# Summing the conv norm's four feature tiles and four squares on VectorE before TensorE sums over partitions

## The chip, the cores and the metric

The kernel runs on one core of a Trainium2 chip. The metric is the device time of one launch in microseconds. Engines: TensorE (PE; its weight loads are PEld), VectorE (DVE), ScalarE (ACT), GpSimd (POOL) and SyncE (SP, whose queue issues the weight transfers). Names after "L" are line numbers of the kernel before.

## The reference

The program computes a first block, then a second block of two layers over 528 positions (16 meta tokens and 512 tokens) of 2048 features. Of each layer of the second block only this matters here:

```
c = c_val * jax.nn.sigmoid(c_glu)
c = _causal_depthwise_conv_2(c, conv_dw_w, conv_dw_b)
c = jax.nn.silu(_layer_norm(c, conv_ln_g, conv_ln_b))
c = c @ conv_pw_w + conv_pw_b
y_conv = c * jax.nn.silu(c_gate)
...
mixed = jnp.concatenate([y_conv, y_attn, y_lru], axis=-1) @ w_out
return _layer_norm(DEEPNORM_ALPHA * h + mixed, ln_post_g, ln_post_b)
```

`_layer_norm` over the 512 conv features takes a mean and then a variance of the centred values. Both are sums over features.

## The kernel before

Activations are held feature-major: a tile is 128 features on the partitions by 528 positions along the free axis, so the 512 conv features are four tiles, y2[:, Y_CONV + d] with d from 0 to 3. A sum over features is a sum over partitions and over four tiles. TensorE does it: `sum_features` (L740) multiplies each tile by a matrix of ones, in two halves of 264 positions, and adds the four tiles up in PSUM. These are plain fp32 matmuls. The large products run as three reduced-precision ones (high times high, low times high, high times low; L513 to L515).

The large products go by "units". A unit is 256 columns of a weight matrix by all positions. It has two passes (m = 0, 1) of four pieces (j = 0 to 3), and a piece in a layer is 24 matmuls of 264 positions. Its weights come by DMA to w_raw, ScalarE makes w_high of them (`high`, L979) and VectorE w_low (`low`, L1471). A piece of the next unit's w_high can be made only when the same piece of this unit's second pass is done (piece_used). Everything is ordered by hand: each engine has its own list, and semaphores join them. Extra work of TensorE is put between pieces by a hook that is called after each piece (n = 0 to 7 in a unit).

The order around the change, in each of the two layers:

- TensorE does unit C (O_CG, the last unit of the loop over groups). After its piece 6 comes the mean (`c_mean`), then piece 7. Then unit C + 1, with the variance (`c_var`) after its piece 0. Then the conv branch's pointwise product PW (L940 to L944), which waits until the normed conv tiles are ready (c_ready) and until all PSUM banks are free (evac), and then six units and a tail of the output product.
- VectorE ends the recurrence of the last group (L1992 to L2003), then `lows(C + 1, range(3))`, then subtracts the mean from the four tiles (L2012), `low(C + 1, 3)`, the reciprocal (L2015), the scaling (L2018) and c_low (L2021).
- ScalarE copies out unit C (L990), makes three pieces of w_high, squares the four centred tiles (L1393), makes the fourth piece, takes the root of the variance (L1397), then silu and c_high for four tiles (L1400, L1402), copies out unit C + 1's first pass (L990), then four times `high(C + 2, j)`, with three pieces of x_high (L1106) between, and then copies out unit C + 1's second pass. That last copy is the evac that PW waits for.

Of the kernel before, what the change touches and what calls it, by code (L numbers as in the profile page):

```python
# [22 lines left out]
ALU = mybir.AluOpType  # L23
# [24 lines left out]
CT = CW // P  # L48
TAPS = 31
HD = 64  # L50
NKV = 4
# [22 lines left out]
O_K, O_V, O_K2, O_GRP, O_CG, O_PW, O_OUT = 0, 1, 2, 3, 19, 21, 22  # L74
# [6 lines left out]
Y_ATT, Y_LRU, Y_CONV = 0, 8, 12  # L81
# [25 lines left out]
def program(nc, a, out):  # L107
# [14 lines left out]
    with ExitStack() as ctx:  # L122
# [92 lines left out]
        y2 = r2.take("y_layer", [P, KT, L])  # L215
# [48 lines left out]
        dif = rn.take("norm_difference", [P, L])  # L264
        dsq = rn.take("norm_square", [P, L])
# [3 lines left out]
        csq = nc.alloc_sbuf_tensor_at("c_square", [P, CT, L], F32, offset=big + 3 * CT * L * 4)  # L269
# [4 lines left out]
        def sem(name):  # L274
            return ctx.enter_context(nc.semaphore(name))
# [47 lines left out]
        c_taken, rw_in, r_conved, r_mm, r_act, r_act2, r_w, r_sqrt, lru_done, pads_ok = (  # L323
            sem("c_taken"), sem("rw_in"), sem("r_conved"), sem("r_mm"), sem("r_act"), sem("r_act2"), sem("r_w"), sem("r_sqrt"),
            sem("lru_done"), sem("pads_ok"))
        zeros_ok = sem("zeros_ok")
        c_gated, c_part, att_sum = sem("c_gated"), sem("c_part"), sem("att_sum")
        lam_exp, sp_ok = sem("lam_exp"), sem("sp_ok")
        cn_mean, cn_c, cn_sq, cn_mm, cn_rt, cn_t, cn_hi, c_ready = (
            sem("cn_mean"), sem("cn_c"), sem("cn_sq"), sem("cn_mm"), sem("cn_rt"), sem("cn_t"),  # L330
            sem("cn_hi"), sem("c_ready"))
# [177 lines left out]
        def _(pe):  # L509
# [29 lines left out]
            def unit(U, fill, wide=False, after=(None, None), mid=(None, None), hook=None, tok=slice(0, S)):  # L539

                for m in range(2):
                    begin(U, m)
                    for j in range(4):
                        arrive(U, m, j, fill)
                        for kt in range(4):
                            k = 4 * j + kt
                            if wide:
                                for q in range(2):  # L550
                                    last = three(ps[:, 2 * m + q, 0:LH], k, None, slice(q * LH, (q + 1) * LH), m, j, kt, k == 0, k == KT - 1)
                            else:
                                last = three(ps[:, m, :], k, None, tok, m, j, kt, k == 0, k == KT - 1)
                        end_piece(U, m, j, last)
                        if j == 1 and mid[m]:
                            mid[m]()
                        if hook:
                            hook(4 * m + j)
                    if after[m]:
                        after[m]()  # L560
# [24 lines left out]
            for d in range(KT):  # L585
                if d >= 4:
                    pe.wait_ge(tr_raw_free, d - 3)
                for i in range(ST):
                    last = pe.transpose(ps[:, 4 + d % 4, i * P:(i + 1) * P], xn[:, i, d * P:(d + 1) * P], ident[:])
# [5 lines left out]
            for d in range(KT):  # L595
# [4 lines left out]
                for i in range(ST):  # L600
                    last = pe.transpose(ps[:, 4 + d % 4, i * P:(i + 1) * P], xs[:, i, d * P:(d + 1) * P], ident[:])
# [5 lines left out]
            for h in range(H):  # L607
                last = pe.transpose(ps[:, 4 + h // 4, h % 4 * P:(h % 4 + 1) * P], ws[:, h, :], ident[:])
            last.then_inc(wst_tr, 1)
            pe.wait_ge(wst_ok, 1)  # L610
            for q in range(2):
                last = pe.matmul(ps[:, 6 + q, :], ones[:], wst[:, 4 * q:4 * q + 4, :], start=True, stop=True)
# [4 lines left out]
            with pe.Fori(0, H) as h:  # L617
                U = U_SGU + 3 * h
# [16 lines left out]
            for i in range(ST):  # L635
                last = pe.transpose(ps[:, 6, i * H:(i + 1) * H], gz[0:H, i * P:(i + 1) * P], ident[0:H, 0:H])
# [3 lines left out]
            with pe.Fori(0, H) as h:  # L640
                U = U_MLSTM + 4 * h
# [35 lines left out]
            for d in range(KT):  # L677
                last = pe.transpose(ps[:, 5, d * NM:(d + 1) * NM], mnat[:, d * P:(d + 1) * P], ident[0:NM, 0:NM])
# [61 lines left out]
            def sum_features(src, n, bank):  # L740

                for d in range(n):
                    for q in range(2):
                        last = pe.matmul(ps[:, bank + q, 0:LH], ones[:], src(d)[:, q * LH:(q + 1) * LH],
                                         start=(d == 0), stop=(d == n - 1))
                return last

            for l in range(LAYERS):
                U = U_LAYER + N_LAYER * l
                fill0 = (3 + 3 * l) * KT  # L750
                fill = fill0 + KT
# [160 lines left out]
                def c_mean(n):  # L912

                    if n != 6:
                        return
                    pe.wait_ge(r_act, 2 * NKV * (l + 1))
                    pe.wait_ge(o_taken, 2 * NKV * (l + 1))
                    pe.wait_ge(c_taken, NKV * (l + 1))
                    pe.wait_ge(mo_ready, 2 * NKV * (l + 1))
                    sum_features(lambda d: y2[:, Y_CONV + d, :], CT, 4).then_inc(cn_mean, 1)  # L920

                def c_var():
                    pe.wait_ge(cn_sq, CT * (l + 1))
                    sum_features(lambda d: csq[:, d, :], CT, 6).then_inc(cn_mm, 1)

                with pe.Fori(0, NKV - 1) as g:
                    group(g)
                group(NKV - 1, c_mean)
                unit(U + O_CG + 1, fill, wide=True, hook=lambda n: c_var() if n == 0 else None)

                pe.wait_ge(c_ready, CT * (l + 1))
                pe.wait_ge(cn_rt, l + 1)
# [1 line left out]
                for t in range(CT):  # L934
                    pe.wait_ge(lo_ready, 4 * (U + O_PW) + t + 1)
                    for k in range(CT):
                        for q in range(2):
                            tok = slice(q * LH, (q + 1) * LH)
                            dst = ps[:, 2 * t + q, 0:LH]
# [4 lines left out]
                            last = pe.matmul(dst, wl[:, t, k, 0:P], chi[:, k, tok], start=False, stop=(k == CT - 1))  # L944
# [6 lines left out]
            for s in range(8):  # L951
# [10 lines left out]
                for k in range(4):  # L962
                    d = 4 * g + k
                    pe.wait_ge(y_full, 2 * KT * LAYERS + KT * q + d + 1)
                    for i in range(2):
                        tok = NM + (2 * q + i) * P
                        last = pe.transpose(ps[:, pairs[s % 3][i], k * P:(k + 1) * P], y2[:, d, tok:tok + P], ident[:])
# [498 lines left out]
        def _(dve):  # L1466

            def low(U, j):

                dve.wait_ge(hi_ready, 4 * U + j + 1)  # L1470
                dve.tensor_tensor(wl[:, j], raw[:, j], f(wh[:, j]), ALU.subtract).then_inc(lo_ready, 1)  # L1471
# [37 lines left out]
            for i in range(ST):  # L1509
                last = dve.tensor_scalar(xs[:, i, :], xn[:, i, :], small[:, 12 + i:13 + i], None, ALU.mult)  # L1510
# [28 lines left out]
            with dve.Fori(0, H) as h:  # L1539
                U = U_SGU + 3 * h  # L1540
# [14 lines left out]
                for i in range(ST):  # L1555
                    last = dve.tensor_scalar(vn[:, i, :], vg[:, i, :], small[:, 40 + 2 * i:41 + 2 * i],
                                             small[:, 56 + i:57 + i], ALU.subtract, ALU.mult)
# [26 lines left out]
            with dve.Fori(0, H) as h:  # L1584
                U = U_MLSTM + 4 * h
# [40 lines left out]
                last = dve.tensor_tensor(ym[:, ds(2 * h, 2), :], ps[:, 4:6, :], rd[:].unsqueeze(1).broadcast_to([P, 2, S]), ALU.mult)  # L1626
# [14 lines left out]
                for c in range(2):  # L1641
                    y = ym[:, ds(2 * h + c, 1), :].squeeze(1)
                    last = dve.scalar_tensor_tensor(y, y, par[:, 0, ds(PR_MNORM + 2 * h + c, 1)], og[:, c, :], ALU.mult, ALU.mult)
# [181 lines left out]
            for l in range(LAYERS):  # L1825
                U = U_LAYER + N_LAYER * l
# [178 lines left out]

                C = U + O_CG
                yc = lambda d: y2[:, Y_CONV + d, :]
                dve.drain()
                lows(C + 1, range(3))
                dve.wait_ge(cn_mean, l + 1)  # L2010
                for d in range(CT):
                    dve.scalar_tensor_tensor(two(yc(d)), halves(4), -1.0 / CW, two(yc(d)), ALU.mult, ALU.add).then_inc(cn_c, 1)  # L2012
                low(C + 1, 3)
                dve.wait_ge(cn_rt, l + 1)
                dve.reciprocal(lrb[:], lrb[:])  # L2015
                dve.drain()
# [100 lines left out]
```

## Time and profile before

| | |
|---|---|
| median of 3 runs | 3503.56 us (3502.77 to 3506.48) |
| the profiled execution's own time | 3504.78 us |
| its span | 3503.2 us |
| PE busy | 3365.1 us, 96% |
| DVE busy | 1743.3 us, 50% |
| ACT busy | 1360.5 us, 39% |
| mean granted TensorE clock | 0.98 of full speed |

The profiled execution took 1.22 us more than the median of the runs, and its span, from the first to the last instruction, is 1.6 us shorter than its own time. Times in the rows are counted from the span's start.

### The profile page before, as it was taken

How to read it: one execution, taken by the hardware profiler on the slowest of the kernel's cores; microseconds unless marked ns; L12 is line 12 of the kernel's file. 1: busy time of each engine (PE TensorE's matmuls, PEld its weight loads, DVE VectorE, ACT ScalarE, POOL GpSimd, SP SyncE). 2: the span in 40 equal slices, each digit the busy share in tenths (PEclk: the TensorE clock that was granted, in tenths of full speed). 3: DMA queues.
4: the chain of work that ended last, by engine and by line, in shares of the span. 5: the costliest groups of instructions: out<-in, count | busy, mean ns of one | idle time of the engine just before them, and what ended most of it. 6: DMA issues, size and time to landing. Idle time of an engine off the chain costs nothing.

```text
span 3503.2 us, 58534 instructions
## 1 busy us (share of the span) xinstructions
PE 3365.1 (96%) x21710; PEld 3048.5 (87%) x21710; DVE 1743.3 (50%) x2523; ACT 1360.5 (39%) x2208; POOL 315.4 (9%) x320
## 2 busy tenths in 40 slices
PE   6999999999999999899978999999997999999997
PEld 5888888888888888788878999999997999999996
DVE  5433233344443434424685555556467455555547
ACT  4323233233333333323244444555225445445424
POOL 2000000000000000000000321430000223312000
PEclk9999999999999999999989999999998999999998
DMA  5322333232323232422224222222324222221422
GB/s 183 96 85 89 90 96 96 79 102 78 102 85 94 79 101 77 137 93 90 93 87 152 67 74 68 68 73 74 138 93 146 88 70 72 74 74 58 146 86 85
DMA packets 359783, 327.47 MB, mean 93 GB/s; under 512 B 19680, under 2 KB 355064, under 8 KB 357696
## 3 DMA queue, kind: packets, MB, share of 16 engines
q1 hardware_dynamic: 352064, 291.58, 27.4%
q10 hardware_dynamic: 3168, 19.18, 1.4%
q0 software_dynamic: 4400, 14.62, 1.2%
q8 instruction: 104, 1.70, 0.2%
q14 instruction: 47, 0.39, 0.0%
HBM read 308.23 MB, written 17.07 MB: 93 GB/s over the span
## 4 chain that ended last, share of the span: by engine, by line
PE 38%; issue 12%; DVE 4%; ACT 3%; DVEq 1%; POOLq 1%; POOL 1%; DMA 0%; ACTq 0%
PE ps L513 11%; PE ps L514 11%; PE ps L515 11%; PE ps L853 1%; PE ps L812 1%; DVE w_low L1471 1%; ACT y_layer L1154 1%; DVE residual L1690 1%; ACT x_high L1156 1%; PE ps L827 0%; DVE residual L1705 0%; PE ps L860 0%; PE ps L884 0%; PE ps L831 0%; DMA residual_stream<-y_layer 0%
## 5 line engine op out<-in xcount | busy, mean ns | idle before, releaser
L513 PE MATMUL ps<-x_high,w_high 128*128 128x264 f32 (+3 forms) x5344 | 1755.0, 328 | 76.2 <-DVE w_low L1471 26.3
L514 PE MATMUL ps<-x_low,w_high 128*128 128x264 f32 (+3 forms) x5344 | 1721.1, 322 | 0.0
L515 PE MATMUL ps<-x_high,w_low 128*128 128x264 f32 (+3 forms) x5344 | 1717.3, 321 | 0.0
L1471 DVE TENSOR_TENSOR w_low<-w_raw,w_high 128x1024 fp32r<-128x1024 f32 x544 | 663.8, 1229 | 1090.5 <-ACT w_high L979 1054.0
L513 PEld LDWEIGHTS ps<-x_high,w_high 128*128 128x128 f32 x5344 | 1016.0, 190 | 165.0 <-issue 68.4
L514 PEld LDWEIGHTS ps<-x_low,w_high 128*128 128x128 f32 x5344 | 1016.2, 190 | 81.8 <-issue 3.8
L515 PEld LDWEIGHTS ps<-x_high,w_low 128*128 128x128 f32 x5344 | 1013.3, 190 | 75.3
L979 ACT ACTIVATE w_high<-w_raw 128x1024 fp32r<-128x1024 f32 x544 | 573.2, 1057 | 746.3 <-PE ps L515 607.2
L519 PE MATMUL ps<-w_high,x_high 128*128 128x256 f32 x1184 | 333.1, 281 | 4.7 <-DVE w_low L1471 2.7
L520 PE MATMUL ps<-w_high,x_low 128*128 128x256 f32 x1184 | 333.3, 282 | 0.0
L521 PE MATMUL ps<-w_low,x_high 128*128 128x256 f32 x1184 | 333.2, 281 | 0.0
L519 PEld LDWEIGHTS ps<-w_high,x_high 128*128 128x128 f32 x1184 | 223.2, 189 | 6.6 <-DVE w_low L1471 3.1
L521 PEld LDWEIGHTS ps<-w_low,x_high 128*128 128x128 f32 x1184 | 223.9, 189 | 0.0
L520 PEld LDWEIGHTS ps<-w_high,x_low 128*128 128x128 f32 x1184 | 223.2, 189 | 0.7
L1904 DVE SCALAR_TENSOR_TENSOR c_partial<-c_raw,par,c_partial 128x528 f32<-128x528 f32 x168 | 141.0, 839 | 30.3 <-issue 30.3
L990 ACT ACT_TABLE_LOAD x86 | 110.3, 1283 | 23.2 <-DVE k_roped L1858 17.7
L444 POOL DMA_DIRECT2D gate_bc<-gate_rows x8 | 4.2, 531 | 1207.1 <-DVE y_m L1626 666.8
L490 POOL TENSOR_TENSOR y_layer<-y_layer,tmp 128x528 f32 x64 | 104.3, 1630 | 9.9 <-issue 9.9
L1872 DVE SCALAR_TENSOR_TENSOR p_block<-ps,shape_constants 128x272 f32<-128x272 f32 x96 | 42.2, 440 | 94.0 <-PE ps L812 90.4
L488 POOL TENSOR_TENSOR tmp<-c_raw,par 128x528 f32<-128x528 f32 x64 | 78.1, 1220 | 14.5 <-issue 14.5
L1154 ACT ACTIVATE y_layer<-residual,par 128x272 f32<-128x272 f32 (+1 forms) x96 | 56.8, 601 | 57.0 <-DVE residual L1705 55.9
L497 POOL TENSOR_TENSOR c_raw<-c_raw,a_gate_silu 128x528 f32<-128x528 f32 x8 | 8.9, 1118 | 716.0 <-ACT a_gate_silu L990 716.0
(335 smaller groups left out, 2657.8 us busy)
## 6 DMA issues: line engine op xcount, KB each, us to landing
w_raw<-in_w_in SPq DMA_DIRECT2D x792, 256.0 KB, 3.0
w_raw<-in_w_out SPq DMA_DIRECT2D x280, 256.0 KB, 3.0
residual_stream<-y_layer ACTq DMA_DIRECT2D x2, 4224.0 KB, 13.6
residual<-residual_stream ACTq DMA_DIRECT2D x8, 1056.0 KB, 10.9
x_natural<-in_x SPq DMA_DIRECT2D x4, 1024.0 KB, 8.9
x_feature_major<-x_stage POOLq DMA_DIRECT2D x16, 256.0 KB, 4.4
gate_bc<-gate_rows POOLq DMA_DIRECT2D x8, 512.0 KB, 4.5
acc<-x_feature_major POOLq DMA_DIRECT2D x1, 4096.0 KB, 13.3
```

The source lines that it names most:

```text
L490: ins = pool.tensor_tensor(ct, ct, t1[:], ALU.add)
L513: pe.matmul(dst, wh[:, j, kt, wc], xh[:, k, tok], start=first, stop=False)
L514: pe.matmul(dst, wh[:, j, kt, wc], xl[:, k, tok], start=False, stop=False)
L515: return pe.matmul(dst, wl[:, j, kt, wc], xh[:, k, tok], start=False, stop=last)
L519: pe.matmul(dst, xh[:, k, tok], wh[:, j, kt, :], start=first, stop=False)
L520: pe.matmul(dst, xl[:, k, tok], wh[:, j, kt, :], start=False, stop=False)
L521: return pe.matmul(dst, xh[:, k, tok], wl[:, j, kt, :], start=False, stop=last)
L979: act.activation(wh[:, j], raw[:, j], ACT.Copy).then_inc(hi_ready, 1)
L990: act.activation(dst, src, fn, **kw).then_inc(evac, 1)
L1154: act.activation(y2[:, d, COLS[q]], r, ACT.Identity, bias=plc(PL_PB + d), scale=plc(PL_PG + d)).then_inc(y_full, 1)
L1471: dve.tensor_tensor(wl[:, j], raw[:, j], f(wh[:, j]), ALU.subtract).then_inc(lo_ready, 1)
L1904: dve.scalar_tensor_tensor(cacc[:], cra[:, j:j + L], wj, cacc[:], ALU.mult, ALU.add)
```

## The change

Before TensorE's sum for the mean, VectorE adds the four conv tiles into one (norm_difference, `dif`). Before the sum for the variance it adds the four squares into one (norm_square, `dsq`). TensorE then multiplies only that one tile by ones. A new semaphore, cn_sum, tells TensorE that the added tile is ready. The three additions of a sum depend on each other and have a drain between them. The variance moves from after piece 0 to after piece 1 of unit C + 1.

```diff
-                    pe.wait_ge(c_taken, NKV * (l + 1))
                     pe.wait_ge(mo_ready, 2 * NKV * (l + 1))
-                    sum_features(lambda d: y2[:, Y_CONV + d, :], CT, 4).then_inc(cn_mean, 1)
+                    pe.wait_ge(cn_sum, 2 * l + 1)
+                    sum_features(lambda d: dif[:], 1, 4).then_inc(cn_mean, 1)
 
                 def c_var():
-                    pe.wait_ge(cn_sq, CT * (l + 1))
-                    sum_features(lambda d: csq[:, d, :], CT, 6).then_inc(cn_mm, 1)
+                    pe.wait_ge(cn_sum, 2 * l + 2)
+                    sum_features(lambda d: dsq[:], 1, 6).then_inc(cn_mm, 1)
...
-                unit(U + O_CG + 1, fill, wide=True, hook=lambda n: c_var() if n == 0 else None)
+                unit(U + O_CG + 1, fill, wide=True, hook=lambda n: c_var() if n == 1 else None)
...
                 yc = lambda d: y2[:, Y_CONV + d, :]
-                dve.drain()
+
+                def add_tiles(dst, src):
+
+                    dve.drain()
+                    dve.tensor_tensor(dst, src(0), src(1), ALU.add)
+                    for d in range(2, CT):
+                        dve.drain()
+                        last = dve.tensor_tensor(dst, dst, src(d), ALU.add)
+                    last.then_inc(cn_sum, 1)
+
+                add_tiles(dif[:], yc)
                 lows(C + 1, range(3))
                 dve.wait_ge(cn_mean, l + 1)
                 for d in range(CT):
                     dve.scalar_tensor_tensor(two(yc(d)), halves(4), -1.0 / CW, two(yc(d)), ALU.mult, ALU.add).then_inc(cn_c, 1)
                 low(C + 1, 3)
+                dve.wait_ge(cn_sq, CT * (l + 1))
+                add_tiles(dsq[:], lambda d: csq[:, d, :])
                 dve.wait_ge(cn_rt, l + 1)
```

On VectorE, before, from the last step of the recurrence (L2003) over the loop's end to the scaling, with the semaphore that a row waits for:

```order
L2003 TENSOR_TENSOR y_layer<-r_tanh,tmp_115 128x528 [waits evac]
L1860 REGISTER_ALU
L1860 COMPARE_AND_BRANCH
L1471 TENSOR_TENSOR w_low<-w_raw,w_high 128x1024 [waits hi_ready] x3
L2012 SCALAR_TENSOR_TENSOR y_layer<-ps,y_layer 128x528 [waits cn_mean]
L2012 SCALAR_TENSOR_TENSOR y_layer<-ps,y_layer 128x528 x3
L1471 TENSOR_TENSOR w_low<-w_raw,w_high 128x1024 [waits hi_ready]
L2015 RECIPROCAL norm_scale_bc<-norm_scale_bc 128x528 [waits cn_rt]
L2018 SCALAR_TENSOR_TENSOR y_layer<-y_layer,par,norm_scale_bc 128x528 x4
```

The same stretch of VectorE in the changed kernel (its lines are numbered one or more higher):

```order
L2004 TENSOR_TENSOR y_layer<-r_tanh,tmp_115 128x528 [waits evac]
L2013 TENSOR_TENSOR norm_difference<-y_layer 128x528
L2016 TENSOR_TENSOR norm_difference<-norm_difference,y_layer 128x528 x2
...
L1472 TENSOR_TENSOR w_low<-w_raw,w_high 128x1024 [waits hi_ready] x3
L2023 SCALAR_TENSOR_TENSOR y_layer<-ps,y_layer 128x528 [waits cn_mean]
L2023 SCALAR_TENSOR_TENSOR y_layer<-ps,y_layer 128x528 x3
L1472 TENSOR_TENSOR w_low<-w_raw,w_high 128x1024 [waits hi_ready]
L2013 TENSOR_TENSOR norm_square<-c_square 128x528 [waits cn_sq]
L2016 TENSOR_TENSOR norm_square<-norm_square,c_square 128x528 x2
L2028 RECIPROCAL norm_scale_bc<-norm_scale_bc 128x528 [waits cn_rt]
```

Three additions now stand ahead of the three w_low pieces, and three behind the fourth piece, ahead of the reciprocal.

On TensorE, at the end of piece 6 of unit C and the start of piece 7, before:

```order
L514 MATMUL ps<-x_low,w_high 128x264
L515 MATMUL ps<-x_high,w_low 128x264
L744 MATMUL ps<-y_layer,ones 128x264 [waits c_taken,mo_ready,o_taken,r_act]
L744 MATMUL ps<-y_layer,ones 128x264 x7
L513 MATMUL ps<-x_high,w_high 128x264
```

The same place in the changed kernel:

```order
L515 MATMUL ps<-x_low,w_high 128x264
L516 MATMUL ps<-x_high,w_low 128x264
L745 MATMUL ps<-norm_difference,ones 128x264 [waits mo_ready,cn_sum,o_taken,r_act]
L745 MATMUL ps<-norm_difference,ones 128x264
L514 MATMUL ps<-x_high,w_high 128x264
```

The sum stands at the same place with two matmuls for eight, and it waits for cn_sum where it waited for c_taken.

## Rows read from the trace of the kernel before

**Rows 1.** The profile's page: busy times and shares of the span

```profile
PE 3365.1 (96%) x21710; PEld 3048.5 (87%) x21710; DVE 1743.3 (50%) x2523; ACT 1360.5 (39%) x2208; POOL 315.4 (9%) x320
```

**Rows 2.** TensorE's waits, 2385 to 2480 us: us in total, times, longest

```profile
PE ps L940 <- ACT c_gate_silu L990: 1.9, 1, 1.9
PE ps L744 <- ACT c_square L1393: 0.3, 1, 0.3
```

**Rows 3.** Line 744, all its matmuls: nanoseconds min/median/max, first and last start

```profile
L744 PE MATMUL ps<-y_layer,ones x32: 383/386/386, 2401.3 to 3230.9; 128*128 128x264 f32 x32
L744 PE MATMUL ps<-c_square,ones x32: 386/386/490, 2411.2 to 3240.9; 128*128 128x264 f32 x32
```

**Rows 4.** Timeline of TensorE, layer one: start, us, instruction, idle before and releaser

```profile
2401.32 3.72 PE L744 MATMUL ps<-y_layer,ones 128*128 128x264 f32 x16
2404.69 0.48 PE L513 MATMUL ps<-x_high,w_high 128*128 128x264 f32 x1
...
2411.15 3.83 PE L744 MATMUL ps<-c_square,ones 128*128 128x264 f32 x16 [0.31 <-ACT c_square L1393]
2414.62 0.48 PE L513 MATMUL ps<-x_high,w_high 128*128 128x264 f32 x1
...
2437.19 0.36 PE L940 MATMUL ps<-c_high,w_high 128*128 128x264 f32 x1 [1.91 <-ACT c_gate_silu L990]
```

**Rows 5.** Timeline of VectorE, the same stretch

```profile
2396.95 0.71 DVE L1992 TENSOR_TENSOR r_conv<-r_conv,y_layer 128x528 f32<-128x528 f32 x1 [5.12 <-ACT r_gate_a L1378]
2397.74 0.71 DVE L1994 TENSOR_TENSOR y_layer<-r_gate_a 128x528 f32 x1
...
2402.13 0.71 DVE L2003 TENSOR_TENSOR y_layer<-r_tanh,tmp 128x528 f32 x1
2404.46 3.50 DVE L1471 TENSOR_TENSOR w_low<-w_raw,w_high 128x1024 fp32r<-128x1024 f32 x3 [1.62 <-ACT w_high L979]
2407.87 2.55 DVE L2012 SCALAR_TENSOR_TENSOR y_layer<-ps,y_layer 128x528 f32<-128x528 f32 x4
2412.08 1.23 DVE L1471 TENSOR_TENSOR w_low<-w_raw,w_high 128x1024 fp32r<-128x1024 f32 x1 [1.66 <-ACT w_high L979]
2415.75 3.45 DVE L2015 RECIPROCAL norm_scale_bc<-norm_scale_bc 128x528 f32<-128x528 f32 x1 [2.45 <-ACT norm_scale_bc L1397]
```

**Rows 6.** Timeline of ScalarE, the same stretch

```profile
2402.87 0.61 ACT L990 ACTIVATE c_gate_silu<-ps 128x528 f32<-128x528 f32 x1 [1.66 <-DVE y_layer L2003]
2403.38 2.94 ACT L979 ACTIVATE w_high<-w_raw 128x1024 fp32r<-128x1024 f32 x3
2408.61 2.49 ACT L1393 ACTIVATE c_square<-y_layer 128x528 f32<-128x528 f32 x4 [2.29 <-DVE y_layer L2012]
...
2415.02 0.70 ACT L1397 ACTIVATE norm_scale_bc<-ps,small 128x528 f32<-128x528 f32 x1 [1.17 <-PE ps L744]
...
2425.48 0.59 ACT L990 ACTIVATE c_gate_silu<-ps 128x528 f32<-128x528 f32 x1
2426.68 1.06 ACT L979 ACTIVATE w_high<-w_raw 128x1024 fp32r<-128x1024 f32 x1 [0.61 <-PE ps L515]
...
2436.35 0.59 ACT L990 ACTIVATE c_gate_silu<-ps 128x528 f32<-128x528 f32 x1
```

**Rows 7.** Stretches: length, busy of PE, PEld, DVE, ACT, POOL, PEclk, DMA share, GB/s

```profile
2438.15:2441.56 3.41, 3.41 (x18) 3.41 (x17) 2.76 (x5) 0.00 (x0) 0.00 (x0) 0.50 0.46 150
2441.56:2449.60 8.04, 8.04 (x69) 8.04 (x68) 4.58 (x5) 5.25 (x6) 0.00 (x0) 1.00 0.36 113
...
3264.17:3267.59 3.42, 3.42 (x18) 3.42 (x17) 3.03 (x5) 0.00 (x0) 0.00 (x0) 0.50 0.51 156
2165.08:2168.49 3.41, 3.41 (x18) 3.41 (x17) 2.07 (x2) 3.36 (x10) 0.00 (x0) 0.50 0.67 202
1883.06:1888.60 5.54, 5.54 (x26) 5.54 (x27) 5.01 (x7) 1.97 (x3) 0.00 (x0) 0.50 0.70 217
```

**Rows 8.** Timeline of TensorE: the waits ahead of those stretches

```profile
3263.48 0.36 PE L940 MATMUL ps<-c_high,w_high 128*128 128x264 f32 x1 [1.91 <-ACT c_gate_silu L990]
...
2164.29 0.39 PE L513 MATMUL ps<-x_high,w_high 128*128 128x264 f32 x1 [2.67 <-DVE w_low L1471]
...
1883.06 0.55 PE L513 MATMUL ps<-x_high,w_high 128*128 128x256 f32 x1 [8.17 <-issue]
```

More of the change, by code:

```diff
@@ L328, in program @@
         lam_exp, sp_ok = sem("lam_exp"), sem("sp_ok")
+        cn_sum = sem("cn_sum")
         cn_mean, cn_c, cn_sq, cn_mm, cn_rt, cn_t, cn_hi, c_ready = (
```

## The prediction

> **What bounds the kernel now.** I read the page first. TensorE is busy for 96% of the span, VectorE for half [rows 1], so work taken from TensorE looks like time won. That share is a mean, so I then read TensorE's waits around the conv norm. Between 2385 and 2480 us there are two: 0.3 us ahead of the variance's sum, for the squares, and 1.9 us ahead of the pointwise product PW (L940), for ScalarE's copy of unit C + 1's second pass [rows 2]. Layer two has the same 1.91 us [rows 8]. So TensorE bounds this stretch except at PW, where the last copy on ScalarE decides. A gain ahead of PW counts only if that copy comes earlier, too, and a delay of that copy counts in full. Third, I followed the copy back on ScalarE. Its last part, from the w_high piece at 2426.68 to the copy at 2436.35, is work of 10.26 us (2436.35 + 0.59 - 2426.68) [rows 6], as long as TensorE's three remaining pieces, and it starts when TensorE has finished a piece, after 0.61 us of idling [rows 6]. That 0.61 us is all the slack that the norm's chain has: root at 2415.02, reciprocal, scaling, silu, copy at 2425.48 [rows 5, 6]. I take TensorE's arrival there as unchanged and come back to it below.
>
> **The change, part by part** (layer one; layer two has the same rows shifted, and all per-layer sums are doubled).
>
> *Removed matmuls.* Each sum is recorded as 16 matmuls; the two layers have 32 for each kind [rows 3]. The mean's 16 start at 2401.32 and the next piece at 2404.69, 3.37 us later; the variance's take 2411.15 to 2414.62, 3.47 us [rows 4]. I take 3.47/16 = 0.217 us for one. A quarter is left, 4 x 0.217 = 0.87 us, so each sum saves 2.60 us, and all four 10.4 us of TensorE.
>
> *Added additions.* The trace of before has no such addition, but it has its like: a VectorE tensor-tensor operation of 128x528 fp32 takes 0.71 us, and two with a drain between start 0.79 us apart (2396.95 and 2397.74) [rows 5]. Three make 2 x 0.79 + 0.71 = 2.29 us. The bounds are near: 3 x 0.71 = 2.13 us below, 3 x 0.79 = 2.37 us above.
>
> *The mean.* The additions follow L2003, which ends at 2402.84 [rows 5]; the first starts at 2402.92 and the last ends at 2405.21. TensorE stands ready at 2401.32 [rows 4], since the sum needed nothing of the recurrence until now. So it waits until 2405.26 (0.05 us for the signal, as from the end of the squares, 2411.10, to 2411.15 [rows 4, 6]): 3.94 us of waiting for 2.60 us saved. Queued behind it are piece 7 of unit C and all of unit C + 1.
>
> *VectorE behind the first additions.* The three w_low pieces used to wait until 2404.46 for w_high, so 1.62 us of idling cover most of the additions [rows 5]. They now start at about 2405.12 (a following operation starts some 0.09 us ahead of the recorded end, as L2012 does at 2407.87), 0.66 us late. Subtraction, squares, the fourth w_high and the fourth w_low are all 0.66 us late, and w_low ends at 2412.08 + 1.23 + 0.66 = 2413.97 [rows 5]. The mean itself is there in time: 2405.26 + 0.87 = 2406.13 against 2408.53.
>
> *The variance.* Before, its sum stood behind the squares alone (2411.10). Now it stands behind w_high, w_low and three additions: 2413.97 + 0.07 + 2.29 = 2416.33, so TensorE starts it at 2416.38. TensorE gets there at 2406.13 + 2.86 (piece 7) + 2 x 2.90 = 2414.79 (a piece is 2.90 us: from 2414.62 to PW's wait at 2435.28 are seven, the last with its drain [rows 4]). So it waits 1.59 us more. The root started 3.87 us after the sum (2411.15 to 2415.02) and will start 3.87 - 2.60 = 1.27 us after it: 2417.65, which is 2.63 us later than before.
>
> *What is late next.* Reciprocal, scaling, silu and c_high follow the root one to one, and the copy moves from 2425.48 to 2428.11. The w_high piece behind it starts some 0.51 us after a copy (2402.87 to 2403.38 [rows 6]): 2428.62 for 2426.68. TensorE releases that piece at 2416.38 + 0.87 + 3 x 2.90 = 2425.95, earlier than ScalarE comes to it. So the slack of 0.61 us is used up, and the last copy and PW's start are late by 1.94 us. TensorE ends unit C + 1 at about 2434.98, 0.3 us earlier than before, and waits 4.15 us there for 1.91 us. The saved matmuls have turned into waiting. Everything behind PW is TensorE's own pace or hangs on PW's results, so nothing takes the delay up: 2 x 1.94 = +3.9 us.
>
> *The clock.* After the 1.91 us of waiting at PW the granted clock is 0.50 for 3.41 us of full work in both layers, so 1.2 instead of 2.4 GHz, and costs half of it, 1.7 us; then it is 1.00 again [rows 7, 8]. After 2.67 us it is the same 1.7 us; after 8.17 us there are 5.54 us of half-clock work, 2.8 us lost [rows 7, 8]. The new wait at the mean should cost as much, but in front of the variance lie 1.59 us of waiting, and ahead of PW 4.15 us, which take 1.7 us up. I cost it at nothing. If that cover were gone it would be 1.7 us a layer. PW's wait of 4.15 us lies between those with 1.7 and 2.8 us lost. It is nearer to 2.67 us, so I take 1.7 us, as before, no difference; the other end is +1.1 us a layer. From below, half-clock time can fall into the longer wait itself, so up to 1.7 us a layer can be won.
>
> The Trainium skill, TensorE: Matmul & The Clock Gate, section "HAM oscillation — how this bites in real kernels", tells of a kernel in which each wait for operands sent the array back to the low clock and was paid for again by the work behind it, every time. It speaks against the change, which makes one more such wait in each layer. By that rule alone the sum would be 3.9 + 2 x 1.7 = 7.3 us by the trace's own price. The trace agrees that a wait as short as 1.91 us is followed by the low clock. It also shows work behind the mean with waits of its own, into which the loss can go, and I stay with 3.9 us.
>
> **The sum.** The profiled execution took 3504.78 us; +3.9 gives 3508.7. Against the median of the runs, 3503.56, the same step gives 3507.5 us, +0.11%. About 0.2%, 7 us, is what a measurement of this kernel can tell from no change.
>
> **The rivals.**
>
> *Faster: the removed matmuls come out.* TensorE is at 96% [rows 1], which speaks for it: 3503.6 - 10.4 = 3493.2 us. It decides at ScalarE's chain: the last copy would have to come earlier with TensorE. Even with free additions it would start only with the root, which would be about 0.3 us earlier, and ScalarE's tail of 10.26 us stays. So I give it little.
>
> *No difference: the norm's chain is later by less than its slack.* If the additions run beside something else or the fourth w_low does not stand in their way, the root is late by at most 0.61 us, PW starts with TensorE's pieces, about 0.3 us earlier: 3503.6 - 0.6 = 3503.0 us. Against it: rows and order put 2.63 us there.
>
> *Slower by more than 0.2%: the new wait's low clock is not taken up.* The mean's wait is followed by half clock for 3.4 us of work, and the delay passes into the norm's chain. It decides if TensorE's lateness exceeds the 1.59 us ahead of the variance, by about its whole size. It costs 1.7 us more in each layer: 3503.6 + 7.3 = 3510.9 us. The same height is reached if PW's longer wait costs 2.8 us in both layers and the median of before had one half-clock stretch less than the profile, as its 1.2 us may mean: 3.9 + 2.1 + 1.2 = 7.2 us.
>
> **How the numbers follow.** My forecast has 0.62, with its own range of 3504.5 to 3510.0 (less 3 us where half clock falls into the waits, more 2.5 us for the clock's other end). No difference has 0.10, slower 0.22, faster 0.06. The range of 8 in 10 leaves out the faster case and the ends: 3502.5 to 3511.5. Chances: faster by over 0.2% 0.05, within 0.2% 0.71, slower by over 0.2% 0.24 (the slower case and the upper end of the forecast's).
>
> **What would show it.** The matmuls on ones should be 4 for 16 at each sum. The mean's should start near 2405.3 for 2401.3, after some 3.9 us of waiting for VectorE's last addition, the variance's near 2416.4 after up to 1.6 us; the root near 2417.7 and PW near 2439.1, about 4 us waited (less what the clock took). Each addition should take 0.71 us and start 0.79 us behind the one ahead. Behind PW's start the granted clock should be 0.50 for some 3.4 us, as before. Wrong would be: ScalarE's piece at 2428.6 still released by TensorE, a variance that starts before the fourth w_low has ended, or a wait behind PW that before did not have or that gets shorter by 1.9 us.

## The result, and the profile after

| | before | after |
|---|---|---|
| median, 20 runs each | 3504.21 us (3502.77 to 3506.52) | 3511.51 us (3509.53 to 3512.89) |
| profiled execution's span | 3503.2 us | 3511.1 us |
| mean granted clock | 0.980 | 0.978 |

The ratio is 1.002, with a 95% interval of 1.0014 to 1.0026: the changed kernel is slower by 7.3 us. The forecast was +3.9 us, the case "slower, the new wait's low clock is not taken up" +7.3 us. The profiled execution of the changed kernel took 3512.75 us, 1.2 us above its median.

The page after, first the busy times (before: [rows 1]):

```profile
PE 3358.8 (96%) x21662; PEld 3044.0 (87%) x21662; DVE 1751.0 (50%) x2535; ACT 1360.5 (39%) x2208; POOL 315.4 (9%) x320
```

TensorE has 48 matmuls fewer and is busy for only 6.3 us less, not 10.4: what is left runs more of its time at half clock. VectorE has twelve additions more, 7.7 us.

TensorE's waits from 2385 to 2480 us (us in total, times, longest; before: [rows 2]):

```profile
PE ps L941 <- ACT c_gate_silu L991: 4.1, 1, 4.1
PE ps L745 <- DVE norm_difference L2016: 3.9, 1, 3.9
```

Both forecast waits are there, 3.9 us at the mean and 4.1 at PW. The one forecast at the variance (up to 1.6 us) is missing. TensorE's timeline shows it too (start, us, instruction, idle before; before: [rows 4]):

```profile
2406.48 2.10 PE L745 MATMUL ps<-norm_difference,ones 128*128 128x264 f32 x4 [3.87 <-DVE norm_difference L2016]
2418.56 1.05 PE L745 MATMUL ps<-norm_square,ones 128*128 128x264 f32 x4
...
2441.09 0.56 PE L941 MATMUL ps<-c_high,w_high 128*128 128x264 f32 x1 [4.07 <-ACT c_gate_silu L991]
```

VectorE, the same stretch (before: [rows 5]):

```profile
2403.26 0.71 DVE L2004 TENSOR_TENSOR y_layer<-r_tanh,tmp 128x528 f32 x1
2404.06 0.71 DVE L2013 TENSOR_TENSOR norm_difference<-y_layer 128x528 f32<-128x528 f32 x1
2404.84 1.49 DVE L2016 TENSOR_TENSOR norm_difference<-norm_difference,y_layer 128x528 f32<-128x528 f32 x2
...
2409.66 2.54 DVE L2023 SCALAR_TENSOR_TENSOR y_layer<-ps,y_layer 128x528 f32<-128x528 f32 x4
2414.11 1.23 DVE L1472 TENSOR_TENSOR w_low<-w_raw,w_high 128x1024 fp32r<-128x1024 f32 x1 [1.91 <-ACT w_high L980]
2415.43 0.71 DVE L2013 TENSOR_TENSOR norm_square<-c_square 128x528 f32<-128x528 f32 x1
2416.21 1.49 DVE L2016 TENSOR_TENSOR norm_square<-norm_square,c_square 128x528 f32<-128x528 f32 x2
```

The squares are added up at 2417.70 (2416.21 + 1.49), and TensorE takes them at 2418.56. It is TensorE that is late, by 0.86 us. ScalarE (before: [rows 6]):

```profile
2410.39 2.49 ACT L1394 ACTIVATE c_square<-y_layer 128x528 f32<-128x528 f32 x4 [2.94 <-DVE y_layer L2023]
2413.02 1.06 ACT L980 ACTIVATE w_high<-w_raw 128x1024 fp32r<-128x1024 f32 x1
...
2419.65 0.70 ACT L1398 ACTIVATE norm_scale_bc<-ps,small 128x528 f32<-128x528 f32 x1 [3.78 <-PE ps L745]
...
2430.11 0.59 ACT L991 ACTIVATE c_gate_silu<-ps 128x528 f32<-128x528 f32 x1
2430.60 1.05 ACT L980 ACTIVATE w_high<-w_raw 128x1024 fp32r<-128x1024 f32 x1
```

ScalarE's w_high piece at 2430.60 stands right behind the copy at 2430.11, without the 0.61 us of idling of before: the norm's chain now decides, as forecast. Last, stretches of time on TensorE (length, busy of PE, PEld, DVE, ACT, POOL, granted clock, DMA; before: [rows 7]):

```profile
2406.48:2411.63 5.15, 5.15 (x19) 4.74 (x20) 5.15 (x7) 2.21 (x5) 0.00 (x0) 0.50 0.41 119
2411.63:2418.56 6.93, 6.93 (x59) 6.93 (x58) 3.92 (x5) 4.09 (x6) 0.00 (x0) 1.00 0.21 63
2441.09:2445.77 4.68, 4.68 (x21) 4.68 (x22) 3.73 (x5) 0.00 (x0) 0.00 (x0) 0.50 0.57 184
```

Behind the mean's wait 5.15 us of work run at half clock (1.2 GHz), which loses 2.6 us; behind PW's 4.68 us, which lose 2.3 us for 1.7 before.

To compare executions, I count from the start of the last recurrence step, VectorE's L2003 in before (2402.13) and L2004 after (2403.26), in layer one. The root was taken 12.89 us behind it and now 16.39: +3.50. PW started 35.06 us behind it (2437.19) and now 37.83: +2.77. Layer two gives +2.75. With 0.62 us more of half-clock loss in each, that is 2.77 + 2.75 + 2 x 0.62 = 6.8 us of the 7.3.

The rest of the kernel bears this out. The spans of the two profiled executions differ by 7.9 us. Of these 1.1 lie ahead of layer one's last recurrence step, where the edit has no part. The other 6.8 us lie behind it, 2.77 and 2.75 of them between that step and PW in the two layers; the half clock behind PW accounts for most of the rest.

### The profile page after: what moved, and what is told of

It reads as the page before. It is cut to its first block, busy times and chain, and to the rows that moved or that the text cites. A ratio compares the mean times of both kernels' runs of the same rounds, so it can differ in the third digit from the quotient of the medians.

```text
span 3511.1 us, 58460 instructions
## 1 busy us (share of the span) xinstructions
PE 3358.8 (96%) x21662; PEld 3044.0 (87%) x21662; DVE 1751.0 (50%) x2535; ACT 1360.5 (39%) x2208; POOL 315.4 (9%) x320
## 4 chain that ended last, share of the span: by engine, by line
PE 38%; issue 12%; DVE 4%; ACT 3%; DVEq 1%; POOLq 1%; POOL 1%; DMA 0%; ACTq 0%
PE ps L514 11%; PE ps L515 11%; PE ps L516 11%; PE ps L854 1%; PE ps L813 1%; ACT y_layer L1155 1%; DVE residual L1691 1%; DVE w_low L1472 1%; ACT x_high L1157 1%; PE ps L828 0%; DVE residual L1706 0%; PE ps L861 0%; PE ps L885 0%; PE ps L832 0%; ACT x_high L1107 0%
```

## The experiments

Three theories are tried. A: the norm's chain sets ScalarE's last copy and with it PW's start, and the low clock behind a wait is part of the cost. B: the same chain, but the low clock costs nothing. C: only TensorE's own time counts, the matmuls saved against the waits added. "Root" is the start of ScalarE's root of the variance, and both it and PW are counted from the recurrence's last step. All runs are compared with runs of the kernel before on the same chip (medians 3504.5 to 3504.8 us); each ratio's interval reaches about 0.0009 to either side (3 us), 0.0013 for the last kernel.

**Only the mean's part.** The variance as before, after piece 0:

```diff
-                    pe.wait_ge(cn_sum, 2 * l + 2)
-                    sum_features(lambda d: dsq[:], 1, 6).then_inc(cn_mm, 1)
+                    pe.wait_ge(cn_sq, CT * (l + 1))
+                    sum_features(lambda d: csq[:, d, :], CT, 6).then_inc(cn_mm, 1)
...
-                unit(U + O_CG + 1, fill, wide=True, hook=lambda n: c_var() if n == 1 else None)
+                unit(U + O_CG + 1, fill, wide=True, hook=lambda n: c_var() if n == 0 else None)
...
-                dve.wait_ge(cn_sq, CT * (l + 1))
-                add_tiles(dsq[:], lambda d: csq[:, d, :])
```

> Only the mean's part of the change: VectorE adds the four tiles, the variance is summed as before, with 16 matmuls after piece 0 of unit C + 1. Theory A (the norm's chain sets PW's start, and the low clock behind the mean's wait is part of what makes it late): TensorE waits 3.9 us at the mean, loses about 2.6 us to half clock behind it, reaches the variance near 2414.5 (for 2411.15, counted as in layer one of before), the root is some 3.3 us late, PW 2.7 us, with 0.6 us more of half clock there: about +6 us against before, 3510. Theory B (the chain without the clock: only VectorE's own 0.66 us is passed on): root 0.75 us late, PW 0.1 us: +0.3 us, 3504.5. Theory C (only TensorE's time counts, waits against savings): 3.94 - 2.60 a layer, +2.7 us, 3507.

Measured: 3512.16 us, ratio 1.002 (1.0011 to 1.0029), +7.6 us, where A had about +6. This half alone costs all that the change costs. TensorE in its trace (start, us, idle before):

```profile
2403.53 0.78 PE L745 MATMUL ps<-norm_difference,ones 128*128 128x264 f32 x1 [3.87 <-DVE norm_difference L2016]
...
2412.78 3.72 PE L745 MATMUL ps<-c_square,ones 128*128 128x264 f32 x16
```

and the stretch behind the wait:

```profile
2403.53:2408.78 5.25, 5.25 (x20) 4.84 (x21) 5.25 (x7) 2.31 (x5) 0.00 (x0) 0.50 0.43 120
```

The root is at 2416.54, 16.23 us behind the recurrence's last step (2400.31), so 3.34 us late; A had 3.3, B 0.75. PW is 3.37 us late, not 2.7: the wait in front of it is 1.94 us as in before, so here TensorE's own lateness reaches it, and the half clock behind it stays at 3.4 us. In the time, theory B (+0.3) falls, and so does C (+2.7).

**Only the variance's part.** The mean is summed as before (cn_sum counts the squares alone):

```diff
-                    pe.wait_ge(cn_sum, 2 * l + 1)
-                    sum_features(lambda d: dif[:], 1, 4).then_inc(cn_mean, 1)
+                    pe.wait_ge(c_taken, NKV * (l + 1))
+                    sum_features(lambda d: y2[:, Y_CONV + d, :], CT, 4).then_inc(cn_mean, 1)
...
-                add_tiles(dif[:], yc)
+                dve.drain()
```

> Only the variance's part: VectorE adds the four squares behind the fourth w_low piece, the sum has 4 matmuls after piece 1; the mean as before. Theory A: no wait at the mean, so no low clock there; the added squares are ready at about 2415.7, TensorE waits 2.4 us for them, the root is 2.0 us late, PW 1.4 us, half clock behind the variance is taken up: +2.7 us, up to +4 with a longer half-clock stretch at PW, 3507 to 3508. Theory B: the same +2.7 us. Theory C: 2.4 us waited for 2.6 us saved, -0.4 us, 3503.8.

Measured: 3504.58 us, 0.9998 (0.9989 to 1.0007). The chain does nearly as forecast: 1.98 us of wait at the variance (2.4 forecast), root 14.79 us behind the recurrence's last step (+1.90), PW +1.16 (1.4 forecast). Yet no time is lost in the median. A's +2.7 us or more is missed; C's 3503.8 lies nearer. Its profiled execution (3508.96 us, the slowest of its 11 runs) has a costly form in layer one, 6.2 us at half clock behind PW for 3.4 before, and a cheap one in layer two, half clock behind the variance, where PW's wait takes it up, and none behind PW. The cheap form pays 1.16 us and saves 1.7. The ten other runs took 3503.2 to 3505.6 us with a mean granted clock of 0.980 or 0.981, the profiled one 0.979. That fits the cheap form in both layers of most of them, but no trace of theirs shows it. By the time alone this run speaks for C; the run with one tile refutes C.

**The additions, unused.** VectorE makes all twelve, TensorE sums as before:

```diff
-                    pe.wait_ge(cn_sum, 2 * l + 1)
-                    sum_features(lambda d: dif[:], 1, 4).then_inc(cn_mean, 1)
+                    pe.wait_ge(c_taken, NKV * (l + 1))
+                    sum_features(lambda d: y2[:, Y_CONV + d, :], CT, 4).then_inc(cn_mean, 1)
...
-                    pe.wait_ge(cn_sum, 2 * l + 2)
-                    sum_features(lambda d: dsq[:], 1, 6).then_inc(cn_mm, 1)
+                    pe.wait_ge(cn_sq, CT * (l + 1))
+                    sum_features(lambda d: csq[:, d, :], CT, 6).then_inc(cn_mm, 1)
...
```

> VectorE makes all twelve additions where the change puts them, but nobody uses them: TensorE sums as before, 16 matmuls each, and waits for what it waited for before. Theories A and B: the squares are 0.66 us late, the additions of squares lie in front of the reciprocal beside TensorE's sum, the root is 0.66 us late and PW hardly at all (0.05 us): +0.1 us, no difference. A theory that VectorE's added work itself is the cost expects +7 us, as the changed kernel.

Measured: 3504.85 us, 0.9999 (0.999 to 1.0008). VectorE's time by itself, when nothing waits for the sums, is not the cost. One detail was wrong: PW came 0.66 us late, not 0.05, since at the variance TensorE itself is 0.65 us late, and so is its release of ScalarE's w_high piece. The 0.61 us of slack helps only where TensorE is not late, too.

**One tile of four.** The change with free additions; the sums leave out three tiles:

```diff
-                    sum_features(lambda d: y2[:, Y_CONV + d, :], CT, 4).then_inc(cn_mean, 1)
+                    sum_features(lambda d: y2[:, Y_CONV + d, :], 1, 4).then_inc(cn_mean, 1)
...
-                    sum_features(lambda d: csq[:, d, :], CT, 6).then_inc(cn_mm, 1)
+                    sum_features(lambda d: csq[:, d, :], 1, 6).then_inc(cn_mm, 1)
...
```

> Leaves out part of the computation: the sums take only the first of the four tiles and of the four squares, so there are 4 matmuls for 16 and no additions; waits as before, variance after piece 1. It is the change with additions that cost nothing. Theories A and B: the root comes 2.6 us earlier, ScalarE's w_high piece is released by the chain again, PW starts 3.3 us earlier, with a longer wait there: -6.6 us, -5.4 with 0.6 us more of half clock a layer, 3498 to 3499. Theory C: -10.4 us, 3493.8.

Measured: 3503.83 us, 0.9996 (0.9987 to 1.0005). With 48 matmuls gone and nothing added, nothing measurable is won. C is refuted: 10.4 us would have shown. A's -5.4 was wrong, too. ScalarE's rows say why:

```profile
2411.19 0.59 ACT L990 ACTIVATE c_gate_silu<-ps 128x528 f32<-128x528 f32 x1
2411.80 1.28 ACT L1397 ACT_TABLE_LOAD   x1
2413.10 0.70 ACT L1397 ACTIVATE norm_scale_bc<-ps,small 128x528 f32<-128x528 f32 x1
```

The root needs a table load of 1.28 us, behind ScalarE's other work, and starts as it ends: 11.73 us behind the recurrence's last step (2401.37), only 1.16 us earlier than before. PW comes 1.89 us earlier, after 5.2 us of waiting, and 6.0 us behind it are at half clock (3.0 us lost for 1.7). That leaves 1.89 - 1.3 = 0.6 us a layer.

**Filler ahead of the mean.** The changed kernel does the old 16 matmuls again, into banks that nobody reads:

```diff
+                    pe.wait_ge(c_taken, NKV * (l + 1))
+                    sum_features(lambda d: y2[:, Y_CONV + d, :], CT, 6)
                     pe.wait_ge(cn_sum, 2 * l + 1)
```

> The changed kernel with the old 16 matmuls of the mean issued again, into PSUM banks 6 and 7 that nothing reads, ahead of the wait for the added tile: TensorE is busy for 3.5 of the 3.9 us. It does more work and uses none of it. Theory A (low clock behind the mean's wait delays the variance): no half clock there, the sum of squares is started when the additions are done, root 2.6 us late instead of 3.5, PW 1.9 instead of 2.8: 1.7 us less than the changed kernel, 3509.8, +5.6 against before. Theory B or C: no gain over the changed kernel, 3511.5 or more.

Measured: 3510.49 us, 1.0017 (1.0008 to 1.0026), +5.7 us where A had +5.6 and the changed kernel has +7.3. The time alone can't tell; the trace can. TensorE's timeline at the mean:

```profile
2403.10 1.16 PE L745 MATMUL ps<-norm_difference,ones 128*128 128x264 f32 x4 [0.23 <-DVE norm_difference L2018]
```

and the stretch that follows, with its granted clock:

```profile
2403.10:2408.00 4.90, 4.90 (x37) 4.77 (x38) 4.90 (x6) 1.95 (x4) 0.00 (x0) 1.00 0.40 109
```

Full clock behind the mean, though TensorE does 3.5 us more work; the root is 15.45 us behind the recurrence's last step, +2.56, where the forecast without a loss of clock was +2.63, and PW +1.82, where it was +1.94. So without the half clock at the mean each step up to PW comes out as forecast. Behind PW the half clock is longer, 6.0 and 5.9 us in the two layers for 3.4 before, which takes 2.5 us back.

**Squares added as they arrive.** The changed kernel with VectorE's additions of squares ahead of the fourth w_low piece:

```diff
+                dve.wait_ge(cn_sq, CT * l + 2)
+                dve.tensor_tensor(dsq[:], csq[:, 0, :], csq[:, 1, :], ALU.add)
+                for d in range(2, CT):
+                    dve.drain()
+                    dve.wait_ge(cn_sq, CT * l + d + 1)
+                    last = dve.tensor_tensor(dsq[:], dsq[:], csq[:, d, :], ALU.add)
+                last.then_inc(cn_sum, 1)
                 low(C + 1, 3)
-                dve.wait_ge(cn_sq, CT * (l + 1))
-                add_tiles(dsq[:], lambda d: csq[:, d, :])
```

> The changed kernel, but VectorE adds the squares as they arrive, ahead of the fourth w_low piece, so that their sum is ready some 3.8 us earlier. Theory A: TensorE, slowed behind the mean's wait, is what comes last at the variance (0.86 us after the sum in the changed kernel), so at most 0.9 us a layer is won at the root (and only if half clock ends earlier): 3511, hardly any difference from the changed kernel. Theory B: the root comes 1.6 us earlier than in the changed kernel at full clock, 3508.

Measured: 3510.82 us, 1.0017 (1.0008 to 1.0027), as A has it. The sum is ready earlier and TensorE comes no sooner: root at +3.50 us in layer one. In layer two it is at +2.64. There the same wait of 3.88 us at the mean is followed by 3.4 us at half clock for 5.1, of which more below.

**The mean's additions in VectorE's gap,** right behind the last conv tile:

```diff
                     dve.tensor_tensor(ct, ct, cacc[:], ALU.add).then_inc(c_taken, 1)
+                    dve.drain()
+                    dve.tensor_tensor(dif[:], y2[:, Y_CONV, :], y2[:, Y_CONV + 1, :], ALU.add)
+                    for d in range(2, CT):
+                        dve.drain()
+                        last = dve.tensor_tensor(dif[:], dif[:], y2[:, Y_CONV + d, :], ALU.add)
+                    last.then_inc(cn_sum, 1)
...
-                add_tiles(dif[:], yc)
+                dve.drain()
```

> The changed kernel, but the tiles of the mean are added right after the last conv tile is written, where VectorE idles for 5.1 us before the recurrence's gates (in the loop over groups, so it is done in every group, and only the last one's result is used). TensorE no longer waits at the mean. Theory A: no low clock there; the variance as in the run with its part alone: TensorE waits 4.9 us for the added squares, root 2.0 us late, PW 1.4 us: +2.7 us, up to +4.5 with half clock behind the longer waits, 3507 to 3508.7. Theory C: mean 2.6 us won, variance 2.3 us lost: -0.6 us, 3503.6.

Measured: 3504.62 us, 1.0 (0.9991 to 1.0009). Without the mean's wait the loss is gone. A's 3507 is missed and C's 3503.6 met, but the chain is late as A says; it is the clock that pays for it. In both layers TensorE waits 3.9 us at the variance, the half clock follows there, and none follows the 2.7 and 2.6 us at PW (PW +2.15 and +1.25, less 2 x 1.7 us: 0.0).

**Both, together.** The edits of the last two runs in one kernel.

> Both of the above: the mean's additions in VectorE's gap, the squares added as they arrive. Theory A: no wait at the mean, 1.0 us at the variance, the root 1.9 us earlier than before, ScalarE's w_high piece 2.6 us earlier, PW 2.5 us earlier, with a longer wait there that costs up to 0.6 us more of half clock: -3.8 to -5 us, 3499 to 3500.4, faster than both kernels. Theory B: -5. Theory C: 10.4 us less of TensorE's work, 1.0 us waited a layer: -8.4 us, 3495.8.

Measured: 3503.69 us, 0.9996 (0.9987 to 1.0005), -1.1 us, where A had -3.8 to -5 and C -8.4. The root is again held by the table load (11.72 and 11.73 us behind the recurrence's last step), PW is 1.9 us earlier, not 2.5, and the half clock behind it lasts 5.7 us for 3.4, which leaves 1.88 - 1.15 = 0.7 us a layer. TensorE's timeline there, then the stretch behind it:

```profile
2436.51 0.56 PE L941 MATMUL ps<-c_high,w_high 128*128 128x264 f32 x1 [4.09 <-ACT c_gate_silu L991]
```

```profile
2436.51:2442.20 5.69, 5.69 (x26) 5.69 (x27) 3.74 (x5) 0.00 (x0) 0.00 (x0) 0.50 0.59 186
```

**Filler at PW.** The changed kernel with 16 unused matmuls in PW's wait:

```diff
+                sum_features(lambda d: f(chi[:, d, :]), CT, 6)
                 pe.wait_ge(evac, 2 * (U + O_PW))
```

> The changed kernel with 16 matmuls that nothing uses, on the ready conv tiles, into banks 6 and 7, ahead of PW's wait for the banks: TensorE works for 3.5 of the 4.07 us that it waits. Theory A: PW starts at the same time, the half clock behind it goes, which costs 4.7 us of 2.35 us a layer: -4.7 us against the changed kernel, 3506.8, +2.6 us against before. If the clock is no part of the cost: 3511.5.

Measured: 3505.09 us, 1.0002 (0.9993 to 1.0011), 6.4 us below the changed kernel. More work, less time: +0.4 us against before, where A had +2.6. TensorE's timeline at PW, then the stretch behind it:

```profile
2440.98 0.39 PE L942 MATMUL ps<-c_high,w_high 128*128 128x264 f32 x1 [0.31 <-ACT c_gate_silu L992]
```

```profile
2440.98:2446.00 5.02, 5.02 (x41) 5.02 (x42) 4.56 (x7) 1.59 (x2) 0.00 (x0) 1.00 0.57 179
```

The half clock behind PW is a cost of its own. 6.4 is more than the 4.7 that the profile has there. Part of the rest is in the trace. In layer one the mean is as in the changed kernel (5.2 us at half clock, root +3.52). In layer two the same wait costs less:

```profile
3234.37:3237.78 3.41, 3.41 (x18) 3.41 (x18) 3.41 (x5) 0.65 (x2) 0.00 (x0) 0.50 0.39 112
3244.44 1.05 PE L745 MATMUL ps<-norm_square,ones 128*128 128x264 f32 x4
3245.53 0.70 ACT L1399 ACTIVATE norm_scale_bc<-ps,small 128x528 f32<-128x528 f32 x1 [3.16 <-PE ps L745]
```

The wait is 3.88 us, the half clock 3.4 us, and the root comes 15.53 us behind the recurrence's last step (3230.00): +2.64, the forecast's +2.63. The layer two of the changed kernel with PW's wait split, below, has the same 3.4 us and +2.67.

**PW's wait split.** The first quarter of PW needs only two banks, which are free long before ScalarE's last copy. The edit, made to three kernels:

```diff
-                pe.wait_ge(evac, 2 * (U + O_PW))
+                pe.wait_ge(evac, 2 * (U + O_PW) - 1)
                 for t in range(CT):
+                    if t == 1:
+                        pe.wait_ge(evac, 2 * (U + O_PW))
```

In the kernel before:

> The kernel before with PW's wait for the PSUM banks split: its first quarter needs only banks 0 and 1, which the copy of unit C + 1's first pass frees; only the second quarter waits for ScalarE's last copy. Theory A (the last copy sets PW's start, the low clock follows the wait): the wait of 1.91 us and the half clock behind it (1.7 us) both go, in both layers: -7.2 us, 3497.4. Theory C (TensorE's own time is the bound, such waits are taken up behind): no difference, 3504.6.

Measured: 3497.15 us, 0.9979 (0.997 to 0.9988), -7.6 us, where A had -7.2 and C nothing. No wait at PW is left and the clock stays full (PW's first row on the timeline, then the stretch):

```profile
2433.59 0.28 PE L942 MATMUL ps<-c_high,w_high 128*128 128x264 f32 x1
```

```profile
2433.59:2445.00 11.41, 11.41 (x97) 11.41 (x96) 10.49 (x13) 7.11 (x9) 0.00 (x0) 1.00 0.51 157
```

In the changed kernel:

> The changed kernel with the same split. Theory A: the wait at the mean and its half clock stay, but TensorE's lateness (0.6 us at the end of unit C + 1) and the last copy (2.8 us late) meet a quarter of PW of 2.9 us: PW's second quarter starts where it did in before, after a wait of some 1.1 us too short for a half-clock stretch: -3.7 us against before, 3500.9, so 3.5 us slower than the kernel before with the split. If the change's cost lay elsewhere than at PW, the split would move the changed kernel by the same 7.2 us as the kernel before, to 3504.3.

Measured: 3500.86 us, 0.9989 (0.998 to 0.9998): 3.7 us slower than the kernel before with the same edit, A had 3.5. With PW's wait split the change costs 3.7 us instead of 7.3; 1.0 us a layer is still waited for the last copy.

And in the kernel with both groups of additions moved:

> Mean's additions in VectorE's gap, squares added as they arrive, and the split wait. Theory A: TensorE comes to PW 4.1 us earlier than before, does the first quarter beside ScalarE's tail, waits some 1.0 us, and the second quarter starts 4.8 us earlier than before, without the half clock: -6.5 us a layer, -13 us, 3491.6. Theory C: 10.4 us less matmul work and 4 us less waiting: -14 us; both theories are near here. If the half clock stays: -9.6 us.

Measured: 3492.45 us (5 runs), 0.9965 (0.9951 to 0.9978), -12.3 us, the fastest kernel here. A had -13. What is left of PW's wait stands ahead of its second quarter:

```profile
2434.21 0.39 PE L943 MATMUL ps<-c_high,w_high 128*128 128x264 f32 x1 [0.97 <-ACT c_gate_silu L993]
```

**Adding up.** For each kernel with PW's wait undivided, and for the kernel before with it split, take from its trace how much later PW starts in the two layers, and add half of what the half clock behind PW lasts longer than before. The changed kernel gives +6.8 us (measured +7.3), the mean's part +6.6 (+7.6), the filler ahead of the mean +6.1 (+5.7), squares added as they arrive +5.5 (+6.1), the mean in the gap 0.0 (-0.2), both -1.5 (-1.1), the filler at PW +0.9 (+0.4), one tile -1.3 (-0.7), the unused additions -0.4 (+0.3), and the kernel before with PW's wait split -7.6 (-7.6). These are within 1.1 us. The variance's part alone is off by more, +2.0 for 0.0. So two quantities, PW's start and the clock behind it, carry the account.

## Why the prediction was right or wrong

The measured 3511.51 us stands on the upper end of the stated range (3502.5 to 3511.5), and the likeliest case was not the one that came. Of 7.3 us the forecast had 3.9.

- *Removed matmuls, added additions:* right. 4 for 16 matmuls, additions of 0.71 us, 0.78 us apart.
- *The mean's wait:* right, 3.87 for 3.94 us, as was the subtraction 0.66 us late.
- *The clock at the mean:* the step that failed. "In front of the variance lie 1.59 us of waiting ... which take 1.7 us up. I cost it at nothing." The half clock covered 5.15 us of work, not 3.4, and lost 2.6 us. (The cover was a little smaller, too: with the mean's wait filled, 1.25 us are waited at the variance.) TensorE came to the variance 0.86 us behind the added squares (2418.56 against 2417.70). It also held up ScalarE's fourth w_high piece, which waits for piece 7 of unit C (0.88 us late for 0.66), and so the added squares by 0.24 us. Root +3.50 for +2.63, PW +2.77 for +1.94: 0.83 us a layer. Filler at the mean brought it back to +2.56 and +1.82. It is the size that failed, not the idea of a cover: where only 3.4 us followed the same wait (layer two of the filler at PW), the cover did take it up and the root was +2.64 us late. The changed kernel's own trace has 5.15 and 5.11 us in its two layers, but it is one execution, above the median; how often a layer has the short form is not shown.
- *The clock at PW:* a term mis-sized, +0.6 us a layer where I took 0. Its upper end of +1.1 held in this kernel, but not with filler at the mean or with one tile (+1.3 in layer one).
- *What is late next:* right in kind. The slack was used up, the last copy decides, nothing behind PW takes the delay up.
- *The rivals:* the slower one is what came, in its place (half clock behind the mean passed into the chain) and height (7.3 us), but by other parts: 2 x (0.83 + 0.6) = 2.9 us, not 2 x 1.7. Its mark, TensorE later than the cover, was met by 0.86 us, not by about the whole 1.7. The faster one is refuted by the run with one tile. My aside there, that with free additions the root would be 0.3 us earlier, was off: 1.16 us, the table load's floor. The case of no difference did not come, for the root was 3.50 us late where its slack is 0.61.
- *The rule of the Trainium skill,* TensorE: Matmul & The Clock Gate, section "HAM oscillation — how this bites in real kernels", that each such wait is paid for again by the work behind it, stands better than I weighed it: the changed kernel's trace has it at both waits in both layers. It does not hold for every wait: with the mean added in the gap, no half clock followed 2.73 and 2.60 us at PW. The sum by that rule, 7.3 us, hit the measured time partly by chance, as the parts show.

In the medians the two halves of the change add up, with 3 us to either side: the mean's costs 7.6 us, the variance's none, both together 7.3. In the chain they do not: the root is 3.34 us late with the one, 1.90 with the other and 3.50 with both. The variance's later additions hide in TensorE's lateness from the mean.

Open: what sets how long the half clock lasts behind a wait, and how much of the runs' spread comes from it. The variance's part alone and the filler at PW each show two forms in one execution, and no run here sets which one comes. A single trace can therefore be off by 1 or 2 us from the median that it explains, and part of what A missed follows from it.

## What to carry to other kernels

Work taken from the busiest engine is won only if the chain that sets its next wait gets shorter too; here nothing measurable was won even with the matmuls gone for free, while splitting one wait by the banks that it really needs won 7.6 us. When a sum moves to another engine, ask what that engine is doing at that moment: the mean's additions cost nothing measurable in a gap of 5.1 us that ends 6 us earlier. Price a new wait of TensorE with the half clock behind it, and don't count on cover that is about as large as the loss.

## What the runs showed of the hardware

- A wait of the same length did not always have the same price. Behind 1.9 us at PW there were 3.4 us of half clock in both layers of before; in the run with unused additions layer one has them and layer two has none:

```profile
3263.39:3268.00 4.61, 4.61 (x38) 4.61 (x39) 4.32 (x6) 1.19 (x2) 0.00 (x0) 1.00 0.56 170
2436.85:2440.26 3.41, 3.41 (x18) 3.41 (x17) 3.23 (x5) 0.00 (x0) 0.00 (x0) 0.50 0.50 162
```

- Half-clock work of 4.7 us (changed kernel) and 5.7 us (both moved) followed waits of the same 4.1 us, and 5.2 or 3.4 us the same 3.9 us at the mean (filler at PW, layers one and two). So the length of a wait does not fix the loss.
- Sixteen useless matmuls in a wait of 4.07 us made the changed kernel 6.4 us faster (3511.5 to 3505.1).
- A table load of 1.28 us ahead of ScalarE's root sets the earliest start of the root: 11.73 us behind the recurrence's last step with one tile, 11.72 and 11.73 with both moved. In the kernel before, ScalarE is done with the load and waits another 1.17 us for TensorE [rows 6].
